# Hybrid attention, convolution and MoE step on one core: second normalisation, router and shared expert reordered by token tile and kept in full float32

## The reference

```python
x = x + gate1 * mix                                   # mix = merged branches @ w_out
h2 = rmsnorm(x, norm2_g) * (1.0 + scale2) + shift2
scores = sigmoid(h2 @ router_w)                       # 64 experts, top 8 of 4 groups of 8
routed = sum over the 8 chosen experts of gate_e * ((silu(h2 @ Wg_e) * (h2 @ Wu_e)) @ Wd_e)
shared = (silu(h2 @ sh_w_gate) * (h2 @ sh_w_up)) @ sh_w_down
x = x + gate2 * (routed + shared)                     # then one last rmsnorm
```

## Time and profile before

| what | value |
|---|---|
| median of 3 runs | 1226.69 us (1225.56 to 1229.65) |
| the profiled execution | 1226.74 us, span 1224.9 us |
| PE busy | 1122.0 us, 92% of the span |
| DVE busy | 1055.0 us, 86% |
| ACT busy | 804.6 us, 66% |
| POOL busy | 234.3 us, 19% |
| moved by DMA | 331.20 MB, mean 270 GB/s |

### The profile page before, as it was taken

One profiled execution on the slowest core, in us unless ns is written; L12 is line 12 of the kernel. 1 busy time (PEld: TensorE's weight loads), 2 busy tenths in 40 slices (PEclk: granted clock), 3 DMA queues, 4 the chain that ended last, 5 costly groups with the idle time before them and its releaser, 6 DMA issues.

```text
span 1224.9 us, 16905 instructions
## 1 busy us (share of the span) xinstructions
PE 1122.0 (92%) x5670; PEld 937.6 (77%) x5670; DVE 1055.0 (86%) x1397; ACT 804.6 (66%) x1000; POOL 234.3 (19%) x182
## 2 busy tenths in 40 slices
PE   4999999979989997787999999999999999999950
PEld 1799999845558896676888888888888888888840
DVE  4769999988994666566999999999999999999987
ACT  6543333777872632326888888888888888888831
POOL 1000000011150010010432232433232332333210
PEclk9899999999999899589999999999999999999985
DMA  9563456644537337328999999999999999999995
GB/s 347 176 169 103 145 171 175 171 128 148 172 73 239 102 101 286 138 102 297 372 382 377 373 361 385 373 377 351 341 350 365 358 377 361 361 372 365 360 388 222
DMA packets 122411, 331.20 MB, mean 270 GB/s; under 512 B 27272, under 2 KB 68839, under 8 KB 97271
## 3 DMA queue, kind: packets, MB, share of 16 engines
q1 hardware_dynamic: 98096, 293.54, 65.3%
q0 software_dynamic: 21296, 32.74, 7.9%
q10 hardware_dynamic: 2968, 4.26, 1.0%
HBM read 328.22 MB, written 43.24 MB: 303 GB/s over the span
## 4 chain that ended last, share of the span: by engine, by line
PE 83%; DVE 7%; ACT 4%; DMA 3%; issue 2%; SPq 0%; ACTq 0%; POOLq 0%; DVEq 0%
PE bank L1652 23%; PE bank L1654 23%; PE bank L1653 22%; PE bank L1662 8%; PE bank L1847 2%; ACT hi L796 2%; PE bank L1835 1%; DMA y_d<-ys,ixt 1%; DVE lo L1130 1%; DMA raw<-in_mod_w_dram 1%; PE bank L1963 1%; PE bank L1668 1%; PE bank L1669 1%; DVE lgu L1524 1%; DVE acc L1562 1%
## 5 line engine op out<-in xcount | busy, mean ns | idle before, releaser
L1524 DVE TENSOR_TENSOR lgu<-raw,hgu 128x2048 fp32r<-128x2048 f32 x128 | 292.0, 2282 | 5.1 <-ACT hgu L1029 5.1
L1029 ACT ACTIVATE hgu<-raw 128x2048 fp32r<-128x2048 f32 x128 | 245.2, 1917 | 4.1 <-issue 4.1
L1652 PE MATMUL bank<-hgu,xgh 128*128 128x512 f32 x512 | 206.3, 403 | 2.8 <-DVE lgu L1524 2.8
L1654 PE MATMUL bank<-hgu,xgl 128*128 128x512 f32 x512 | 200.9, 392 | 0.0
L1653 PE MATMUL bank<-lgu,xgh 128*128 128x512 f32 x512 | 199.5, 390 | 0.0
L1531 DVE TENSOR_TENSOR lo<-raw,hi 128x2048 fp32r<-128x2048 f32 x64 | 147.8, 2310 | 25.6 <-ACT hi L1038 20.1
L1130 DVE TENSOR_TENSOR lo<-raw,hi 128x2048 fp32r<-128x2048 f32 (+3 forms) x61 | 133.4, 2189 | 36.6 <-ACT hi L796 36.6
L754 POOL DMA_INDIRECT xg<-h_d,ixt x64 | 66.7, 1041 | 397.1 <-DVE gsl L1496 388.5
L763 POOL DMA_INDIRECT y_d<-ys,ixt x64 | 128.3, 2005 | 57.9 <-ACT ys L1070 38.1
L1228 DVE SCALAR_TENSOR_TENSOR zb<-zb,cwt 128x400 f32<-128x400 f32 x240 | 135.7, 638 | 0.6
L796 ACT ACTIVATE hi<-raw 128x2048 fp32r<-128x2048 f32 (+3 forms) x61 | 111.5, 1830 | 32.6 <-PE bank L1654 21.4
(11 more groups left out here) (292 smaller groups left out, 2139.4 us busy)
## 6 DMA issues: line engine op xcount, KB each, us to landing
raw<-in_exp_w_gate_dram SPq DMA_DIRECT2D x64, 1024.0 KB
raw<-in_exp_w_up_dram SPq DMA_DIRECT2D x64, 1024.0 KB
raw<-in_exp_w_down_dram SPq DMA_DIRECT2D x64, 1024.0 KB, 10.7
raw<-in_mod_w_dram SPq DMA_DIRECT2D x20, 1024.0 KB, 5.2
raw<-in_w_in_dram SPq DMA_DIRECT2D x16, 512.0 KB, 5.5
raw<-in_w_in_dram SPq DMA_DIRECT2D x8, 1024.0 KB, 5.4
mraw<-in_mod_w_dram SPq DMA_DIRECT2D x4, 1024.0 KB, 15.8
raw<-in_w_o_attn_dram SPq DMA_DIRECT2D x4, 1024.0 KB, 5.0
```

The lines of the kernel that those rows point to most:

```text
L1029: act.activation(hgu[k % 2][:, :, w, :], src, ACT.Copy).then_inc(ghi_done, 1)
L1524: dve.tensor_tensor(lgu[k % 2][:, :, w, :], src, hgu[k % 2][:, :, w, :].bitcast(F32), ALU.subtract).then_inc(glo_done, 1)
L1652: pe.matmul(out, ah, bh, start=first, stop=False)
L1654: return pe.matmul(out, al, bh, start=False, stop=last)
```

## The change

What it does:
- `h2p` is written in plain column order; ACT makes the regrouped copy `h2g` for the DRAM rows. h2 is transposed tile by tile (8 transposes, two ACT copies to `h2T`), is not split, and router and shared gate/up run as plain float32 matmuls. Router and shared weights leave `front_items`: they are loaded whole, unsplit (`wr`, `shw`).
- PE's order becomes: transposes of tile 0, router 0, half of shared gate/up 0, transposes 1, router 1, a quarter of shared 0, transposes 2, router 2, the last quarter, shared 1, positions, shared 2, lists 0 and 1, transposes of shared hidden rows 0 and 1.
- ACT does tile 0's copies before the squares of tiles 1 and 2; the root takes scale and bias itself; DVE normalises tile 0 before it sums tiles 1 and 2.
- The shared down product moves behind the expert loop, plain float32, from `shT` kept in SBUF into six PSUM banks that DVE adds directly (`plus_shared`). `sh_d`, `shy` and their transfers go; a 1 MB load of the down weights takes the place of the 1.5 MB `rowsh`.
- The last two experts' rows have buffers and semaphores of their own (`ys_last`, `scattered_last`).
- Small tiles are placed elsewhere; waits on `sh_out` and `h2d_out` in ACT's stream go.

```diff
-    it += [("router",), ("shgu", 0), ("shgu", 1), ("shd",)]
...
+def matmul_order():
+    g = psum_groups()
+    g = g[:g.index(("h2T", 0, 0))]
+    g += [("h2T", 0, 0), ("h2T", 0, 1), ("rt", 0), ("shgu", 0), ("h2T", 1, 0), ("h2T", 1, 1), ("rt", 1)]
+    g += [("h2T", 2, 0), ("h2T", 2, 1), ("rt", 2), ("shgu", 1), ("pos",), ("shgu", 2)]
+    g += [("list", 0), ("list", 1)] + [("shT", t) for t in range(NT)]
...
# SP
+            sp.dma_start(wr[:, :, :], router_w[0].rearrange("(k p) n -> p k n", p=P)).then_inc(wr_in, 16)
+            got(sp, ("wout", 0, 2))
+            for h in range(2):
+                for w, src in enumerate((sh_w_gate, sh_w_up)):
+                    sp.dma_start(shw[h][:, :, FF * w:FF * w + FF],
+                                 src[0, 512 * h:512 * h + 512, :].rearrange("(k p) n -> p k n", p=P)).then_inc(shw_in[h], 16)
...
+            load_gate_up(0, 1, parts=(0,))
             sp.wait_ge(h2_done, NT)
-            load_gate_up(0, 1)
+            load_gate_up(0, 1, parts=(1,))
             load_gate_up(0, 2)
-            sp.wait_ge(shy_done, 2 * NT)
-            sp.dma_start(sh_d, shy[:, :, :]).then_inc(sh_out, 16)
...
-            sp.wait_ge(sh_out, 16)
-            sp.dma_start(tb["sh"][0][2][:, :, :], sh_d).then_inc(row_in["sh"], 16)
+            sp.dma_start(shd[:, :, :], sh_w_down[0].rearrange("(p k) n -> p k n", k=2)).then_inc(shd_in, 16)
...
# POOL
-                pool.wait_ge(h2_done, t + 1)
-                pool.dma_start(h2_d[t * P:(t + 1) * P, :], h2p[:, t, :]).then_inc(h2d_out, 16)
+                pool.wait_ge(h2g_done, t + 1)
+                pool.dma_start(h2_d[t * P:(t + 1) * P, :], h2g[:, t, :]).then_inc(h2d_out, 16)
...
-            got(pool, ("shgu", 2))
...
# ACT
+            mean_square2(0)
+            turned2(0)
+            mean_square2(1)
+            mean_square2(2)
             gate_up_hi(0, 0, 0)
+            turned2(1)
+            turned2(2)
+            for t in range(NT):
+                scores(t)
             gate_up_hi(0, 0, 1)
...
+                regrouped2(t)
+            for t in range(NT):
+                shared_act(t)
+            shared_turned(0)
+            shared_turned(1)
+            turn_hi(0, 0)
+            shared_turned(2)
             act.wait_ge(x1_out, 16)
...
-            act.wait_ge(sh_out, 16)
             act.dma_start(fgr[:, :], final_g.rearrange("(a n) -> a n", a=1).partition_broadcast(P)).then_inc(tail_in, 16)
...
# ACT, rows_out
-                if from_step(j, 2):
+                if from_step(j, 2) and not last:
                     act.wait_ge(scattered[k % 2], uses(i, k - 2) * 16)
...
# DVE
+            for t in range(NT):
+                residual(0, t)
+            scales2()
+            residual(1, 0)
+            normed2(0)
+            residual(1, 1)
+            residual(1, 2)
+            normed2(1)
+            normed2(2)
+            gate_up_lo(0, 0, 0)
...
             list_of(0, 0)
             list_of(0, 1)
+            shared_hidden(0)
+            shared_hidden(1)
...
-            gate_up_lo(0, 0, 0)
             gate_up_lo(0, 0, 1)
             onehot(0, 2)
+            shared_hidden(2)
+            turn_lo(0, 0)
             onehot(0, 3)
-            turn_lo(0, 0)
             list_of(0, 2)
...
-            for n in (3, 4, "sh"):
+            for n in (3, 4):
                 for t in range(NT):
                     plus(n, t)
+            for t in range(NT):
+                plus_shared(t)
...
# PE
+            turn2(0)
+            pe.wait_ge(wr_in, 16)
+            route(0)
+            p = begin(("shgu", 0))
+            shared_part(p, 0, 0, 2)
+            turn2(1)
+            route(1)
+            shared_part(p, 0, 2, 3)
+            turn2(2)
+            route(2)
+            shared_part(p, 0, 3, 4)
+            p = begin(("shgu", 1))
+            shared_part(p, 1, 0, 4)
             pe.wait_ge(mask_done, 1)
             p = begin(("pos",))
...
+            sh2 = begin(("shgu", 2))
+            shared_part(sh2, 2, 0, 4)
...
             token_list(0, 0)
             token_list(0, 1)
+            turn_shared(0)
+            turn_shared(1)
...
             turn_tokens(0, 0)
+            pe.wait_ge(*read_by(("list", 1)))
             token_list(0, 2)
+            turn_shared(2)
...
+            pe.wait_ge(shd_in, 16)
+            for t in range(NT):
+                if t == 2:
+                    pe.wait_ge(ys_done, before_last)
+                for b in range(2):
+                    for k in range(2):
+                        ins = pe.matmul(psum[shared_banks[t][b]][:, :], shT[t][:, P * k:P * k + P],
+                                        shd[:, k, 512 * b:512 * b + 512], start=(k == 0), stop=(k == 1))
+                ins.then_inc(sh_filled, 1)
```

318 lines of the change are left out of this document (142 added, 176 removed).

## The result

| | before | after |
|---|---|---|
| median of the runs, us | 1227.41 (1225.56 to 1229.65, 4 runs) | 1208.6 (1207.24 to 1209.9, 4 runs) |
| profiled execution, us | 1226.74 | 1209.21 |
| its span, us | 1224.9 | 1207.4 |

The ratio is 0.9846, with a 95% interval of 0.9825 to 0.9867. Faster, as forecast, and clear of the spread of the runs, but by 18.8 us (1.5%) where 29.0 were forecast, and 0.6 us above the upper end of the range.

The account below looks back on a forecast made before the run. PE was taken as the bound, over two thirds of the chain being `mm3`, with the loop's 9.67 us step unchanged. Sum: 1226.74 - 24.3 - 11.0 + 1.7 + 4.6 = 1197.7 us, range 1189 to 1208.

Parts of the forecast that it names:

- the lists behind all shared matmuls: Before the loop: PE makes the lists only after all shared gate/up matmuls, which was said to cost 4 us.
- part 2: From the stored lists to the loop: gather, transposes, copies and weight pass, forecast at 10.6 us, 11.0 us less than before.
- part 1: From the projection to the lists: lists stored at 517.5 instead of 541.85, a gain of 24.3 us.
- wait 497.5, router 499.2. So scores are complete at 499.5: PE's third router, after tile 2's transposes: waits until 497.5, ends at 499.2; scores complete 19.2 us earlier.
- I take 4.9, since ... the queues are near empty: First gather, issue to landing: 4.9 us taken from 4.9 to 10.8, as SP waits for a split.
- The edge of 10.8: Upper end of the gather's 4.9 to 10.8 us from issue to landing, priced at 5.9 us in a rival.
- 1.7 us of low clock in part 1: Allowance for short PE waits around the routers before the lists: one spell of 3.4 us at half speed.
- some 4 us: Tail: time after which PE's high clock was expected back during the shared down matmuls.
- So I date the loop by this row: Loop start dated by DVE's first weight split at 563.50, since DVE then runs without pause until PE leads.
- Part 3: Tail: late down weights, PE at low clock, DVE waiting; +4.6 us, bounds -4.5 and +13.
- Rival A: Clock falls for some 15 us of the shared stage, or gather takes 10.8: 1204 to 1212; chance 0.17.

Follow-up runs that it names:

- e3: Changed kernel with PE making lists 0 and 1 after half of tile 2's shared gate/up instead of all of it; median 1205.94 us, ratio 0.9829.
- e1: Changed kernel with ScalarE's scores of tiles 0 and 1 ahead of its copy of tile 2's transposes; median 1205.66 us, ratio 0.9828.
- e18: Changed kernel with SP's load of expert 2's up weights issued only after the first gather has landed; median 1208.3 us, ratio 0.9859.
- e2: Changed kernel with DVE's second weight remainder pass of expert 0 ahead of the first two list reads; median 1204.5 us, ratio 0.9819.
- e10: Changed kernel with 7 unread 512-column matmuls on PE while it waits for expert 0's gathered rows; median 1207.34 us, ratio 0.9836.
- e13: Changed kernel with the split of expert 0's down weights moved from the loop's first steps into the gather's wait; median 1205.51 us, ratio 0.9826.
- e16: Kernel of seven combined edits (1194.58 us) with three unread 384-column matmuls in PE's wait ahead of expert 2's gate/up; median 1191.16 us, ratio 0.9714.
- e4: Changed kernel with SP's load of the shared down weights issued before the fifth row load in the tail; median 1201.1 us, ratio 0.9798.
- e17: Combined edits plus early down-weight split (1190.3 us), with unread matmuls in PE's waits for gathered rows and expert 1's transposes; median 1186.44 us, ratio 0.9677.
- e7: Changed kernel with 14 unread 512-column matmuls on PE in its wait for expert 0's gathered rows; median 1213.49 us, ratio 0.9893.
- e14: Kernel of seven combined edits (1194.58 us) with three unread 384-column matmuls one expert too late, where PE waits for nothing; median 1196.95 us, ratio 0.976.

## Why the prediction was wrong

Right: what bounds the kernel, the loop's step of 9.67 us, the projection's end and h2 (tile 0 at 483.4, forecast 483.2), the place and the mechanism of the tail, and, roughly, that the lists behind all shared matmuls cost 4 us (3.4 in e3). Wrong was the start of the loop: the step of the prediction that failed is part 2, 11.0 us forecast from the lists to the loop and 2.4 measured, and behind it part 1 with 24.3 forecast and 20.4 measured.

- **Part 1, "wait 497.5, router 499.2. So scores are complete at 499.5": 2.5 us missed.** I had ScalarE's scores on no one's path but DVE's. They free the bank of the third router, and they stood behind the copy of tile 2 and a table load of 1.28 us. e1 shows it. With the low clock that followed this is 3.15 us of the 3.9 that the lists missed.
- **Part 2, "I take 4.9, since ... the queues are near empty": 3.2 us missed.** It was 8.10. The issue itself took 3.17 us beside DVE's pass (1.7 us too long), and the buffer that this pass freed brought SP's next load beside the rows (2.1 us; e18). Together e2 gives 3.9 us up to the gate/up. The edge of 10.8 covered the size without naming a cause.
- **Part 2, PE cold.** I allowed 1.7 us of low clock in part 1, at the routers. There it was 1.4 us (10.17 against 8.80), and 0.4 in the third router (2.35 against 1.97). No row of the kernel before gives the length of that spell, 3.4 us, or the "some 4 us" of the tail; the rows after show the clock at 0.50 from 501 to 504, and in the tail from PE's start at 1166.36 to 1170. But the stretch behind the gather's wait, where PE idles for 7.46 us, was priced at the high clock: transposes 1.94 us in place of 1.0, first gate/up at half speed for its first part. e10, with the clock kept up there, brings the gate/up 1.96 us nearer.
- **"So I date the loop by this row".** Before, that pass was late for a reason of its own, ScalarE's issue of `fgr`, and PE's first gate/up ran 3.1 us ahead of it (560.36 against 563.50). The change removed that reason, so that the row moved by 27.25 us and PE's first gate/up by 23.3. By the forecast's own numbers PE's row gave 560.36 - 527.5 = 32.9 us where DVE's gave 35.4: 2.5 us were counted that could not be had. The trace after agrees: before, DVE ran without a pause from 563.50 on, and PE waited for it; now DVE stands idle for 1.20 and 1.31 us (543.87, 545.67), because ScalarE waits for PE's first gate/up. DVE no longer bounds the start, PE does. Then DVE's passes held PE for 2.81 us at expert 2, and the clock fell behind that, 1.6 us (e13, e16); before, PE's waits for DVE in these steps came to as much (0.44, 1.13 and 1.69 us), so that this wait is no loss against before, only the clock is.
- **Part 3, +4.6, measured +5.3.** The mechanism and the size were right: weights late behind `row`, PE cold, DVE waiting. e4 shows that the order of two loads is worth 7.1 us.

The sum: 3.9 at the lists, 8.6 from there to expert 5, 0.7 in the tail, less the 1.7 allowed for the clock, is 11.5 of span. The 8.6 are 5.6 up to the gate/up (15.64 us behind the lists, forecast 10.0: 0.7 until the gather's issue, 3.2 for the gather, 1.7 from the rows to the gate/up), 2.5 for the row that dated the loop, and 0.5 from the gate/up to expert 5 (37.34 against 36.83). Rival A's range, 1204 to 1212, holds the measured 1208.6. It had half the mechanism (a low clock and a slow gather), but its low clock stood at the shared matmuls, where it cost 1.4 us and not 7.5; that its number fits is luck.

## What to carry to other kernels

Date a pipeline's start by the engine that bounds its steady state, not by the row that looks latest: a row late for a reason that the change removes moves farther than the loop does. A wait of PE can be paid twice, once as it stands and once in half-speed matmuls behind it; where nothing useful can be moved into it, matmuls whose result nobody reads can be cheaper (medians 3.4 and 3.9 us lower in e16 and e17), but only if the time won isn't lost at the next wait (e10), they don't outlast the wait (e7), and there is a wait (e14). Before a gather is issued on the critical path, look at what VectorE runs at that moment.
